# Two transformer blocks on one Trainium2 core: reordering the mixer stage (inverse masks, slab pieces, sequence steps, attention by token, early modulation dots)

## The reference, cut to what matters

```python
h = rms_norm(x, norm1_g);  proj = h @ w_in                 # 6 pairs of 256-column slabs
xa, ga, q, k, v, fl, pc = split(proj)
# RWKV-7: token shift, low-rank decay/gate, then per head and token
#   state = state * w + (state @ -kk) b^T + v k^T;  o = state @ r
# RG-LRU: conv of width 4, two gates, h_t = a_t h_(t-1) + b_t, gelu(gate) * h, rms_norm
# forgetting attention, 8 heads of 64: q,k are rms-normed per head
s = q @ k.T * scale + c[q] - c[k];  p = softmax(causal(s));  o = rms_norm(concat(p @ v))
x = x + concat(ya, yb, yc) @ w_out;  x = x + hier_moe(rms_norm(x, norm2_g))
# second block
mod = silu(c) @ w_ada + b_ada                              # 6 x 1024 numbers per layer, 2 layers
```

## Time and profile before

| | us |
|---|---|
| median of 3 executions (2987.88 to 2989.75) | 2987.92 |
| profiled execution | 2987.01 |
| its span, first to last instruction | 2985.2 |
| PE busy | 2758.9 (92%) |
| DVE busy | 1517.7 (51%) |
| ACT busy | 1094.2 (37%) |
| POOL busy | 906.2 (30%) |

### The profile page before, as it was taken

The page is one execution under the profiler, slowest core; times in us unless marked ns, Lnnn a source line. Parts: engine busy times, 40 slices in busy tenths (PEclk is TensorE's granted clock), DMA queues, the critical chain, the costliest instruction groups (busy, mean ns, idle before and its releaser), DMA issues.

```text
span 2985.2 us, 34203 instructions
## 1 busy us (share of the span) xinstructions
PE 2758.9 (92%) x13238; PEld 2259.9 (76%) x13238; DVE 1517.7 (51%) x1696; ACT 1094.2 (37%) x1231; POOL 906.2 (30%) x200
## 2 busy tenths in 40 slices
PE   7787887899998999999899999899999998999998
PEld 5576555688877888887777888678988877778886
DVE  5743577679973431145137676534311351476756
ACT  3321234367753343233333222233442333332222
POOL 3210101100003234434333444332344343334443
PEclk9899878889999999999999999999999999999999
DMA  6110002659952222222234444322232222344443
GB/s 267 57 35 23 8 29 101 230 214 372 366 187 84 71 71 98 94 89 101 85 119 148 148 183 162 138 73 69 71 107 98 86 94 89 113 148 152 178 162 127
DMA packets 65321, 376.67 MB, mean 126 GB/s; under 512 B 7728, under 2 KB 8752, under 8 KB 29872
## 3 DMA queue, kind: packets, MB, share of 16 engines
q1 hardware_dynamic: 63040, 368.58, 34.2%
q10 hardware_dynamic: 2160, 6.42, 0.6%
...
## 4 chain that ended last, share of the span: by engine, by line
PE 71%; issue 4%; DVE 3%; POOL 2%; ACT 2%; DMA 1%; ACTq 0%; DVEq 0%; SPq 0%; POOLq 0%
PE pd L239 17%; PE pd L241 17%; PE pd L240 17%; POOL sb_w_lo L217 2%; PE pd L260 2%; PE pd L259 2%; PE pd L258 2%; PE pd L1679 2%; PE pd L1681 2%; PE pd L1680 2%; PE pd L1706 1%; PE pd L1708 1%; PE pd L1707 1%; DMA sb_ada_held<-in_ada 1%; ACT sb_w_hi L208 1%
## 5 line engine op out<-in xcount | busy, mean ns | idle before, releaser
L217 POOL TENSOR_TENSOR sb_w_lo<-sb_raw,sb_w_hi 128x2048 fp32r<-128x2048 f32 x189 | 891.5, 4717 | 1857.1 <-ACT sb_w_hi L208 1857.1
L239 PE MATMUL pd<-sb_h_hi,sb_w_hi 128*128 128x512 f32 x1696 | 680.7, 401 | 49.7 <-DVE sb_h_lo L336 25.6
L240 PE MATMUL pd<-sb_h_lo,sb_w_hi 128*128 128x512 f32 x1696 | 668.6, 394 | 0.0
L241 PE MATMUL pd<-sb_h_hi,sb_w_lo 128*128 128x512 f32 x1696 | 667.6, 394 | 0.0
L208 ACT CAST sb_w_hi<-sb_raw 128x2048 fp32r<-128x2048 f32 x189 | 360.9, 1909 | 320.2 <-PE pd L241 314.6
L239 PEld LDWEIGHTS pd<-sb_h_hi,sb_w_hi 128*128 128x128 f32 x1696 | 324.1, 191 | 130.4 <-DVE sb_h_lo L336 29.7
L239 PE MATMUL pd<-sb_y_hi,sb_w_hi 128*128 128x512 f32 x960 | 376.4, 392 | 27.3 <-issue 17.0
L241 PEld LDWEIGHTS pd<-sb_h_hi,sb_w_lo 128*128 128x128 f32 x1696 | 323.5, 191 | 69.1
L240 PE MATMUL pd<-sb_y_lo,sb_w_hi 128*128 128x512 f32 x960 | 375.7, 391 | 0.0
L241 PE MATMUL pd<-sb_y_hi,sb_w_lo 128*128 128x512 f32 x960 | 375.5, 391 | 0.0
L240 PEld LDWEIGHTS pd<-sb_h_lo,sb_w_hi 128*128 128x128 f32 x1696 | 324.0, 191 | 67.8 <-issue 2.2
...
## 6 DMA issues: line engine op xcount, KB each, us to landing
...
```

Source lines behind the costliest of these rows:

```text
L217: pool.tensor_tensor(w_lo[j][:], raw[j][:], w_hi[j][:].bitcast(F32), ALU.subtract).then_inc(w_lo_ready[j], 1)
L239: pe.matmul(out, w_hi[j][:, cols], hi[:, k], start=(k == 0), stop=False)
L240: pe.matmul(out, w_hi[j][:, cols], lo[:, k], start=False, stop=False)
L241: last = pe.matmul(out, w_lo[j][:, cols], hi[:, k], start=False, stop=(k == KT - 1))
```

## The change

What it does, in the order of the kernel:

- The row c and 6 dot tiles are loaded right behind slab 0, slab 1 and then the other 12 tiles before slabs 2 and 3. ACT makes the silu before it splits slab 0. DVE does 6 dots ahead of the norm's reciprocal; the other 12 stand before the shifts 0, 2, 4 and 6, as 2, 4, 4 and 2.
- Inverse: PE does second_products(n) first and then all pieces of the step; DVE does mask(n+2) before update(n), as soon as first_product(n) is over (`ct_x`).
- Sequence: DVE's reciprocals are spread over the chunks, one of 256 columns behind a chunk at most. LRU's exponentials move to chunk 0 on ACT. q and k are normalised in place by one DVE operation a tile, and ACT copies them into the per-head tiles (`per_head`). The spreads start at chunk 5, and two of them, two normalisings, four ACT copies and one root lie behind the last chunk. The LRU scans move into attention's units 1 to 3.
- Attention: units go by query block, the largest first, then by head. The probabilities are not scaled. The transposed probabilities are the stationary operand, so the output is by token (128 tokens x 64), and ACT copies it with the reciprocal of the row sum as a scale (`weighted_out`). The norm goes by block: ACT's squares with row sums, one root for two blocks, DVE's scaling by token, 4 transposes and one multiplication by the gain. Two blocks are done within the units, two behind them. 10 dots instead of 12.
- Output projection: 20 dots, as 7, 8 and 5, with 8 tiles' room instead of 4; slab 14 is loaded first, slab 15 behind 8 dot tiles.

```diff
-ADA_FIRST, ADA_FOX, ADA_HELD, ADA_SLOTS = 18, 12, 4, 12
+ADA_BEFORE, ADA_FIRST, ADA_FOX, ADA_HELD = 6, 18, 10, 4
+ADA_LATE = (7, 8, 5)
...
-        o_att = M[:, 14:18]
-        sq_qk, sq_att = W[:, 12:16], Y[:, 2:6]
+        o_tok, o_sq = M[:, 14:18], M[:, 18]
+        sq_qk = W[:, 12:16]
         qk_rstd = T[0:16, 3]
         spread = W[0:16, 10:12].rearrange("p a n -> p (a n)")
-        fl_a, fl_b = T[0:8, 2], T[0:8, 3]
+        fl_a, fl_b = M[0:8, 0], M[0:8, 1]
...
-        UNITS = [(h, qb) for h in range(8) for qb in range(TB)]
+        UNITS = [(h, qb) for qb in (3, 2, 1, 0) for h in range(8)]
...
-            for j in range(2):
-                sp.dma_start(raw[j][:], t["slabs"][j]).then_inc(raw_loaded[j], 16)
+            sp.dma_start(raw[0][:], t["slabs"][0]).then_inc(raw_loaded[0], 16)
+            sp.dma_start(c_row_first, t["c_row"].partition_broadcast(P)).then_inc(c_row_first_loaded, 16)
+            for n in range(ADA_BEFORE):
+                sp.dma_start(ada_first[n], t["ada"][n]).then_inc(ada_first_loaded[n // 3], 16)
+            sp.dma_start(raw[1][:], t["slabs"][1]).then_inc(raw_loaded[1], 16)
             sp.dma_start(c1[:], t["c1"]).then_inc(c_loaded, 16)
             sp.dma_start(blk[:], t["blk"]).then_inc(c_loaded, 16)
             sp.dma_start(ident[:], t["ident"]).then_inc(c_loaded, 16)
-            for j in range(2):
-                sp.wait_ge(w_lo_ready[j], 1)
-                sp.dma_start(raw[j][:], t["slabs"][2 + j]).then_inc(raw_loaded[j], 16)
-            sp.dma_start(c_row_first, t["c_row"].partition_broadcast(P)).then_inc(c_row_first_loaded, 16)
-            for n in range(ADA_SLOTS):
+            for n in range(ADA_BEFORE, ADA_FIRST):
                 sp.dma_start(ada_first[n], t["ada"][n]).then_inc(ada_first_loaded[n // 3], 16)
-            for j in range(2):
-                sp.wait_ge(w_lo_ready[j], 2)
-                sp.dma_start(raw[j][:], t["slabs"][4 + j]).then_inc(raw_loaded[j], 16)
-            for n in range(ADA_SLOTS, ADA_FIRST):
-                sp.wait_ge(ada_used, n - ADA_SLOTS + 1)
-                sp.dma_start(ada_first[n - ADA_SLOTS], t["ada"][n]).then_inc(ada_first_loaded[n // 3], 16)
+            for m in range(1, 3):
+                for j in range(2):
+                    sp.wait_ge(w_lo_ready[j], m)
+                    sp.dma_start(raw[j][:], t["slabs"][2 * m + j]).then_inc(raw_loaded[j], 16)
...
+                second_products(n)
                 k = FILL[n % 5]
-                fill(n, k, 1)
-                second_products(n)
-                if FILL[n % 5 + 1] > k + 1:
-                    fill(n, k + 1, 1)
+                fill(n, k, FILL[n % 5 + 1] - k)
...
-                if c >= 4:
-                    qk_spreads(2 * (c - 4) + place)
+                if c >= 5:
+                    qk_spreads(2 * (c - 5) + place)
...
-            pe.wait_ge(qk_ready, 8)
+            qk_spreads(6)
+            qk_spreads(7)
...
-                pe.wait_ge(sc_prob, n + 1)
+                pe.wait_ge(sc_exp, n + 1)
...
+                if n >= 2:
+                    pe.wait_ge(o_out, n - 1)
+                else:
+                    pe.wait_ge(ln_cen, n + 1)
                 for b in range(qb + 1):
-                    last = pe.matmul(px[2 + pair % 2][rows, qb * P:(qb + 1) * P],
-                                     v_att[:, b, h * 64:(h + 1) * 64], probsT[:, n % 4, b * P:(b + 1) * P],
-                                     start=(b == 0), stop=(b == qb), skip_group_check=True)
+                    last = pe.matmul(px[2 + n % 2][:, 0:CH], probsT[:, n % 4, b * P:(b + 1) * P],
+                                     v_att[:, b, h * CH:(h + 1) * CH], start=(b == 0), stop=(b == qb))
                 last.then_inc(sc_pv, 1)
+
+            def turn_block(i, bank):
+                pe.wait_ge(fox_scaled, i + 1)
+                for k in range(4):
+                    last = pe.transpose(bank[:, k * P:(k + 1) * P], o_tok[:, i, k * P:(k + 1) * P], ident[:])
+                last.then_inc(fox_turned, 1)
...
+            act.wait_ge(c_row_first_loaded, 16)
+            act.activation(c_row_first, c_row_first, ACT.Silu).then_inc(c_row_first_ready, 1)
             split(act, 0, 0)
...
+            def per_head(n):
+
+                act.wait_ge(qk_norm, n + 1)
+                if n < 4:
+                    if n == 0:
+                        act.wait_ge(qz_zero, 1)
+                    act.copy(qz(2 * n)[0:64], q_raw[0:64, n])
+                    act.copy(qz(2 * n + 1)[64:128], q_raw[64:128, n]).then_inc(qk_ready, 1)
+                else:
+                    act.copy(kz(2 * n - 7), k_att[:, n - 4]).then_inc(qk_ready, 1)
+
+            def lb_root(j):
+
+                act.wait_ge(lru_sqrt_in, j + 1)
+                act.activation(lb[:, j], lb[:, j], ACT.Sqrt, scale=2.0).then_inc(lru_b, 1)
...
+                if c >= 5:
+                    per_head(2 * (c - 5))
+                    per_head(2 * (c - 5) + 1)
+            per_head(6)
+            per_head(7)
+            lb_root(1)
...
+            def weighted_out(n):
+                h, i = UNITS[n][0], n // 8
+                act.wait_ge(sc_pv, n + 1)
+                act.wait_ge(sc_inv, n + 1)
+                act.activation(o_tok[:, i, h * CH:(h + 1) * CH], px[2 + n % 2][:, 0:CH], ACT.Copy,
+                               scale=small[:, 40 + n % 4:41 + n % 4]).then_inc(o_out, 1)
+                if h == 7:
+                    act.wait_ge(o_out, n + 1)
+                    act.activation(o_sq, o_tok[:, i], ACT.Square,
+                                   accum_out=small[:, 44 + i:45 + i]).then_inc(fox_sq, 1)
+
+            def block_roots(i):
+                act.wait_ge(fox_sq, i + 2)
+                act.activation(small[:, 48 + i:50 + i], small[:, 44 + i:46 + i], ACT.Sqrt, bias=EPS,
+                               scale=1.0 / 512).then_inc(fox_root, 1)
...
                 if n == 20:
+                    block_roots(0)
+                if n == 22:
                     act.wait_ge(y_lru, 2)
                     split_next(act, IN1_PAIRS - 1, 1)
...
+            dve.wait_ge(c_row_first_ready, 1)
+            ada_begin(0, ADA_BEFORE)
+            dve.wait_ge(ada_used, ADA_BEFORE)
             norm_vector(dve, v, 0, M[:, 0:8], lambda k: v1("norm1", k))
...
+                if n % 2 == 0:
+                    ada_begin(*((6, 2), (8, 4), (12, 4), (16, 2))[n // 2])
...
             for n in range(TB * INVERSE_LEVELS):
+                if n + 2 < TB * INVERSE_LEVELS:
+                    dve.wait_ge(ct_x, n + 1)
+                    mask(n + 2)
                 update(n)
-                if n + 2 < TB * INVERSE_LEVELS:
-                    mask(n + 2)
...
+                to, gain = (q_raw[:, n], small[:, 30:31]) if n < 4 else (k_att[:, n - 4], v1("fox_kn"))
+                v(dve.scalar_tensor_tensor(to, to, gain, pd[n % 4][:], ALU.mult, ALU.mult), qk_norm, n + 1)
...
             def behind_w(c):
+                if c == 2:
+                    lb_one(1)
+                if c == 4:
+                    lru_input(0)
                 if c == 5:
+                    normalise(0)
                 if c == 6:
+                    normalise(2)
+                if c == 7:
+                    lb_product(1)
+            def behind_u(c):
+                if c == 3:
+                    lb_product(0)
+                if c == 4:
+                    lru_input(1)
+                if c == 5:
+                    normalise(1)
+                if c == 6:
+                    normalise(3)
                 if c == 7:
                     normalise(4)
+            def behind_s(c):
+                if c == 1:
+                    lb_one(0)
+                    lb_over(0, 0)
+                if c == 2:
+                    lb_over(0, 1)
                 if c == 3:
+                    qk_inverse(0)
                 if c == 4:
+                    qk_inverse(1)
                 if c == 5:
+                    lb_over(1, 0)
                 if c == 6:
+                    lb_over(1, 1)
                 if c == 7:
                     normalise(5)
...
+            normalise(6)
+            normalise(7)
             dve.wait_ge(seq_o, NCH)
-            for j in range(2):
-                lru_run(j)
...
+            def scale_block(i):
+                v(dve.tensor_scalar(o_tok[:, i], o_tok[:, i], small[:, 52 + i:53 + i], None, ALU.mult), fox_scaled, i + 1)
+            def block_inverses(i):
+                dve.wait_ge(fox_root, i // 2 + 1)
+                v(dve.reciprocal(small[:, 52 + i:54 + i], small[:, 48 + i:50 + i]))
+            def block_out(i, bank):
+                dve.wait_ge(fox_turned, i + 1)
+                b = UNITS[8 * i][1]
+                gain = vec[:, V1["fox_norm"]].unsqueeze(2).to_broadcast([P, 4, P])
+                v(dve.tensor_tensor(Y[:, 2:6, b * P:(b + 1) * P], bank[:].rearrange("p (k n) -> p k n", k=4), gain,
+                                    ALU.mult), y_fox, i + 1)
...
```

(62 more changed lines are left out.)

237 lines of the change are left out of this document (97 added, 140 removed).

## The result

The changed kernel takes 2919.19 us (median of 4 runs, 2916.45 to 2920.72) beside 2987.9 us (2986.02 to 2989.75) for the kernel before on the same chip: a ratio of 0.977, 95% interval 0.9754 to 0.9785. The forecast was 2920. The profiled execution took 2918.53 us, its span 2916.7 us; the mean clock is 0.957.

A forecast was written before the change was run, and what follows sets the result against it. Three stages were taken as chains between engines, not full engines; in attention DVE was busiest but for PE. Terms summed to -67.6 us against 2987.01, 2919.4, with the median 0.9 higher: 2920, range 2896 to 2944.

The forecast's parts named there:

- Head: Stages up to the inverse: norm starts later, low-rank products 7.6 us earlier; -11 us, bounds +8 and -14.
- the bare sum: Head: the shifts added up without POOL's collisions, -12.5 us; the forecast took -11.
- Inverse: Inverse stage: PE's own work sets the step, 100.6 us instead of 134.6; -34, bounds -36 and 0.
- The rival (half of the gain): Inverse: mask or X still ends last in half of the steps, half of 34 lost; 2937 us, chance 0.10.
- the slower one (lower clock): Inverse: PE's work pays fully for the lower clock, up to +99.6 us; 3019 us, chance 0.03.
- Sequence: Sequence's chunks: long reciprocal stalls go, lower clock from chunk 4, chunks 5 to 7 stay 12.1 us; -9.
- into attention: From last chunk to first exponential: added spreads, normalising, copies, root and table take 12.5 us; +4.5, bounds +1 and +7.
- Attention's body: First exponential to last unit's product: 79 us instead of 87.7; -8.7, bounds +3 and -15.
- 14 (79 - 65): Attention's body: lumps +9 (DVE, units 13 to 18) and +6 (ACT), less 1 overlap, on PE's 65 us.
- The rival "attention gives nothing": Lumps at units 13 to 22 lower the clock, attention stays 87.7 us, head gives -3; 2937 us, chance 0.16.
- Tail: Behind attention's last product: 8.0 us instead of 13.8, mostly a long reciprocal before; -5.8, bounds -3 and -7.5.
- projection: Output projection: DVE's queue with 5 dots last ends at 562.1 instead of 565.74; -3.6, bounds 0 and -6.3.

The follow-up runs named there:

- e7: The changed kernel without attention's three long DVE reciprocals, so LRU's and RWKV's norms are left out: 2913.3 us, ratio 0.976 to the kernel before.
- e1: The changed kernel with both edits of the inverse (DVE's order, PE's order) taken back: 2956.0 us, ratio 0.9901 to the kernel before.
- e3: The changed kernel with PE's order in the inverse alone taken back, DVE's early mask kept: 2924.8 us, ratio 0.9791 to the kernel before.

## Why the prediction was right, and where its terms were not

- **Head, -11 against -8.0.** The reciprocal (28.59) and the low-rank products (88.84) came out within 0.5 us, DVE's chain at -10.8 where the bare sum said -12.5 and the forecast -11. The loss is behind it, in a stretch to which the forecast gave no term: from the chain to the inverse it is 66.4 us before, 69.2 after, 66.2 in e7, whose code there is the same as the changed kernel's, at mean clocks of 0.95, 0.90 and 0.95. Of the ten traces with the new head and no collision of DVE with POOL, five have 69.1 to 69.2 us at 0.90, three 66.2 and two 67.6 to 67.7 at 0.95; the two with the old head have 66.4. So the 2.8 us are a state of the clock that comes and goes with the same code. Whether the new head makes it more frequent stays open.
- **Inverse, -34 against -36.5**, half a microsecond beyond its bound. The plain sum of PE's work was right (99; with the 1.70 us of its own row for the second products, where it used 1.75, it is 98.0), and the 1.5 us for masks beside POOL were not needed. e1 shows that 35.0 us are the edits' own; e3 that the mask two steps ahead alone gives nine tenths of them. The rival (half of the gain) and the slower one (lower clock) are both refuted: the clock was 1.00.
- **Sequence, -9 against -10.8; into attention, +4.5 against +2.1.** The mechanism was right, down to 12.1 us for chunks 5 to 7 and, in e3, 12.3 for the way in at the lower level. The clock rose in the middle of the way in, where I had kept it down.
- **Attention's body, -8.7 against -4.2: the mis-sized term.** One price in it was too low: "with 64 moving columns instead of 128 I take 0.15 us a block instead of 0.245". PE's timeline of one unit with four blocks, from the start of the product with v to the start of the next operation, first of the kernel before, then of the changed one:

```profile
458.60 1.09 PE L811 MATMUL px<-sb_M,sb_xT 128*64 128x128 f32 x8
459.62 1.13 PE L786 MATMUL pd<-sb_xT,sb_H 128*128 128x512 f32 x2
```
```profile
384.42 1.00 PE L822 MATMUL px<-sb_xT,sb_M 128*128 128x64 f32 x8
385.26 0.86 PE L800 MATMUL pd<-sb_W,sb_H 128*128 128x384 f32 x2
```

1.02 us for four blocks before, 0.84 after: 0.21 us a block, against the 0.15 taken, so 80 blocks save 3.6 us of PE and not 7.6. What had been left out is the stationary side: the probabilities are now loaded as 128 columns instead of 64, and a load takes 192 ns instead of 137. The row of the changed kernel's loads (minimum, median, maximum in ns; before, 132/137/232):

```profile
L822 PEld LDWEIGHTS px<-sb_xT,sb_M x160: 186/192/338, 361.8 to 439.6; 128*128 128x128 f32 x160
```

That loads set the pace fits these rows, but no run tests it. And this price is not what made the forecast of the stage too short, because the sum did not use it. Its 2.67, 2.09 and 1.52 us for units of four, three and two blocks are the pitch with the old product: of 2.67, the scores (0.96), the gates (0.22) and a product of 1.02 leave 0.47 for four transposes, and at 0.15 us a block it would be 2.25. In the changed kernel, where nothing holds PE up, a unit of four blocks takes 2.41 us from start to start:

```profile
371.02 1.08 PE L800 MATMUL pd<-sb_xT,sb_H 128*128 128x512 f32 x2
...
373.43 1.08 PE L800 MATMUL pd<-sb_W,sb_H 128*128 128x512 f32 x2
```

Three blocks take 1.86 and two 1.32. So PE's work at the upper clock had been put too high. But the body ran at a mean clock of 0.85, and PE's waits sum to 17.1 us where the forecast had left 14 (79 - 65). The other 66.3 us stand against its 65, and the two differences make the error. PE's waits by cause (us in total, times, longest), the largest of the body before and after:

```profile
PE px L796 <- DVE sb_M L1335: 11.5, 11, 3.4
```
```profile
PE px L822 <- ACT sb_M L1062: 11.4, 10, 4.2
```

All causes together are 17.4 us before and 17.1 after: the wait for DVE's scaling went, and one for `weighted_out` came. The exponentials say where. Units 13 to 18 take 21.6 us instead of 20. Units 24 to 30, with the two turned blocks among them, take 10.0 instead of some 8.6. From the last exponential to the end of the last product it is 3.9 us instead of 1.1, because ACT loads the root's table ahead of its last two copies:

```profile
437.09 1.28 ACT L1085 ACT_TABLE_LOAD   x1
...
439.01 1.09 PE L822 MATMUL px<-sb_xT,sb_M 128*128 128x64 f32 x4 [1.27 <-ACT sb_M L1062]
```

These rows give 5.8 us too much against an error of 4.5; the first 13 units gave some of it back. How the error divides is read from rows, not shown by an experiment. ACT's roots at 11 and 20 were sized well (+6; 4.2 and 2.3 above the pitch around them), though I had not seen that DVE would wait for them through `weighted_out`. The rival "attention gives nothing" was half right: the gain is half of the forecast's, and the clock did fall among the lumps (0.56, 0.50 and 0.57 in the windows from 407 to 422). Its other half, the head at -3, did not come.
- **Tail, -5.8 against -7.2; projection, -3.6 against -2.9.** Both within their bounds. The eight transposes took 1.94 us where I had put up to 3.6, and the root's table load of 1.28 us came in the body instead of here.

The prediction was thus right in its total partly by luck: six errors of 1 to 4.5 us went both ways. What was not luck is that the largest term was argued from PE's own durations and came within 3 us.
